# Two score products instead of three in the differential heads of a two-layer encoder, by rows copied between partitions

## The chip, the cores and the metric

The kernel runs on one core of a Trainium2 chip. The metric is the device time of one execution in microseconds (us). The kernel before took 2270.39 us (median of three executions, 2268.04 to 2270.62).

## The reference

Two layers (`L`) are applied with the same weights to two requests of 512 positions and width 1024. Per layer:

```
h = rms(x) * attn_norm;  z = h @ w_in                  # dq, dk, dv, c_q, c_kv, k_pe
dq, dk = rope(dq), rope(dk)                            # 4 heads, 2 components of 64 each
p = softmax(dq_c . dk_c / 8), c = 0, 1;  a = p_0 - lam * p_1
y_diff = rms(a @ dv) * subln                           # differential attention, 4 heads
y_mla = latent attention from c_q, c_kv, k_pe          # 4 heads, 128 + 64 wide
x = x + [y_diff, y_mla] @ w_o
x = x + (silu(h' @ w_gate) * (h' @ w_up)) @ w_down     # h' = rms(x) * ffn_norm
```

## The kernel before

All products are float32 in two parts: `x = hi + lo`, where `hi` is the rounded value and `lo` what is left. `product` (line 526) makes a product of three matmuls, hi·hi, hi·lo and lo·hi (lines 528, 529 and 530), added up in one PSUM bank. ScalarE makes the `hi`, VectorE the `lo`.

A layer does its attention for request 0, then for request 1 (a half each, called l and b in the code; there are four), and then the feed-forward part for both. Each engine does a half in an order written out by hand: `TENSOR_ORDER`, `SCALAR_ORDER` and `VECTOR_ORDER` (lines 71 to 108). An engine takes its steps strictly in that order and waits in each for semaphores. The steps that matter here:

- `P q1` is the projection of the queries of head 1, 8 products or 24 matmuls of 128x512. `Pa` and `Pb` are its two halves of 12 matmuls. `RP` (VectorE, line 1904) rotates its result into `r1` in four operations, `RH` (ScalarE, `rope_his`, line 1437) makes the `hi` part, `RL` (VectorE, `rope_los`, line 1920) the `lo` part.
- `S i` are the scores of a block of 128 queries (line 1140): for i below 16, differential head i // 4, its two components as two products of 128x512, so six matmuls. `MX i` (VectorE, line 2043) takes their row maxima, `EX i` (ScalarE, line 1476) their exponentials, `CB i` (VectorE, line 1994) puts the two components together, `T i` transposes on TensorE, `TH i` and `TL i` split that into hi and lo, `A a` applies it to the values. `S 16` to `S 31` are the latent heads. The score banks are three: a score waits for the exponential of the third one before it.
- `RQ`, `ST`, `RB` and `AP` belong to the norms of the heads' outputs.

A head's q and k projections come out with their 128 rows in four blocks of 32: component 0 first half, component 1 first half, component 0 second half, component 1 second half (`_pair`, line 2380). The queries of component c are kept in `qd[..][c]` as hi and lo with the rows of the other component at zero (a mask in `RH` and `RL`); the keys are kept once, in `kd` as hi and lo. So in each score matmul half of the 128 rows are zeros on the query side.

Weights come in DMAs of 1 MB (`w<-parked`, line 619) on SyncE's queue, each when a slot comes free. In the first half of layer 0 they come raw and are split by ScalarE and GpSimd while the half runs (`slot_hi` on line 1519, line 864). At the ninth chunk of a request 1 half, SyncE also stores request 0's `x` in one DMA of 2 MB (`keep_x`, line 636). ScalarE issues five DMAs, all in the first 16 us.

Of the kernel before, what the change touches and what calls it, by code (L numbers as in the profile page):

```python
# [66 lines left out]
def order(text):  # L67
# [4 lines left out]
    V | P q0 | P k0 | P q1 | S 0 | Pa k1 | S 1 | Pb k1 | T 0 | S 2 | Pa q2 | S 3 | T 1 | Pb q2 | Pa k2 | S 4 | T 2 | A  # L72
    0 | S 5 | Pb k2 | T 3 | Pa q3 | A 1 | S 6 | T 4 | Pb q3 | ST y0 | S 7 | T 5 | P k3 | S 8 | T 6 | Pa kpe | A 2 | S
    9 | Pb kpe | T 7 | RB y0 | Pa ckv | S 10 | A 3 | T 8 | S 11 | Pb ckv | T 9 | ST y1 | S 12 | T 10 | Pa cq0 | RB y1
    | S 13 | Pa cq1 | ST ckv | T 11 | Pb cq0 | S 14 | RB ckv | Pb cq1 | S 15 | ST cq | A 4 | T 12 | RB cq | T 13 | A 5
    | T 14 | P kn0 | P pe0 | P qn0 | T 15 | ST y2 | A 6 | A 7 | S 16 | P vm0 | S 17 | P vm1 | S 18 | P vm2 | RB y2 | P
    vm3 | T 16 | P kn1 | ST y3 | P qn1 | S 19 | P kn2 | RB y3 | S 20 | P pe1 | S 21 | T 17 | S 22 | P qn2 | T 18 | A 8
    | S 23 | P kn3 | P oa0 | T 19 | P qn3 | T 20 | A 9 | S 24 | S 25 | S 26 | S 27 | T 21 | P oa1 | S 28 | T 22 | P
    oa2 | T 23 | A 10 | S 29 | T 24 | S 30 | A 11 | T 25 | P oa3 | T 26 | P oa4 | T 27 | S 31 | A 12 | T 28 | A 13 |
    ST n | T 29 | P oa5 | T 30 | P oa6 | T 31 | A 14 | A 15 | P oa7 | P ob0 | P ob1 | P ob2 | RB n | P ob3 | P ob4 | P  # L80
    ob5 | P ob6 | P ob7
""")
SCALAR_ORDER = order("""
    V | RH q0 | RH k0 | EX 0 | EX 1 | RH q1 | TH 0 | EX 2 | TH 1 | RH k1 | EX 3 | TH 2 | EX 4 | RH q2 | EX 5 | TH 3 |
    YC 0 | TH 4 | RH k2 | EX 6 | RH q3 | TH 5 | EX 7 | TH 6 | EX 8 | RH k3 | TH 7 | EX 9 | EX 10 | SH y0 | TH 8 |
    YC 1 | TH 9 | EX 11 | LC ckv | TH 10 | EX 12 | RH kpe | SH y1 | TH 11 | EX 13 | EX 14 | SH ckv | LC cq0 | LC cq1 |
    TH 12 | EX 15 | TH 13 | SH cq | YC 2 | PH kn0 | TH 14 | PH qn0 | TH 15 | RH pe0 | EX 16 | PH vm0 | PH vm1 |
    PH vm2 | YC 3 | PH vm3 | PH kn1 | SH y2 | EX 17 | TH 16 | PH qn1 | EX 18 | EX 19 | SQ 0 | PH kn2 | SQ 1 | TH 17 |
    SH y3 | EX 20 | SQ 2 | TH 18 | PH qn2 | RH pe1 | PH kn3 | EX 21 | TH 19 | PH qn3 | EX 22 | EX 23 | EX 24 | TH 20 |
    YC 4 | EX 25 | EX 26 | TH 21 | TH 22 | EX 27 | TH 23 | TH 24 | SQ 3 | SQ 4 | YC 5 | TH 25 | EX 28 | TH 26 |  # L90
    EX 29 | EX 30 | SQ 5 | SQ 6 | TH 27 | SQ 7 | SN 0 | TH 28 | SN 1 | SN 2 | TH 29 | EX 31 | SN 3 | SN 4 | SN 5 |
    TH 30 | YC 6 | TH 31 | YC 7 | SN 6 | SN 7
# [40 lines left out]
def numbered(names):  # L133
    return {n: i for i, n in enumerate(names)}
# [4 lines left out]
ROPED = numbered([s[1] for s in VECTOR_ORDER if s[0] == "RP"])  # L139
ROPE_SPLITS = numbered([(n, c) for n in ROPED for c in range(2 if n[0] in "qp" else 1)])  # L140
# [130 lines left out]
def encoder_trunk(nc, xT, watt, wffn, tables, gains, lam, out):  # L271
    with ExitStack() as ctx:
        KB = 1024
# [67 lines left out]
        kd = [[at(f"kd{n}_{s}", [P, T], r_qk + (n * 12 + 8 + i * 2) * KB, F32R)  # L341
               for i, s in enumerate(("hi", "lo"))] for n in range(2)]
# [65 lines left out]
        def sem(name):  # L408
            return ctx.enter_context(nc.semaphore(name))
# [48 lines left out]
        s_rope_lo = Count(sem("rope_lo"), len(ROPE_SPLITS))  # L458
        s_latent = Count(sem("latent_copied"), len(LATENT))
# [544 lines left out]
        def _(pe):  # L1004
# [135 lines left out]
            def scores(l, b, i):  # L1140
                h, qt = i // NT, i % NT
                at_q = slice(qt * P, (qt + 1) * P)
                for c in range(2 if i < 16 else 1):
# [243 lines left out]
        def _(act):  # L1387
# [49 lines left out]
            def rope_his(l, b, name):  # L1437
# [365 lines left out]
        def _(dve):  # L1803
# [676 lines left out]
```

## Time and profile before

| | us |
|---|---|
| median of three executions | 2270.39 |
| the profiled execution | 2269.12 |
| its span, first to last instruction | 2267.3 |
| TensorE busy | 2232.9 (98%) |
| VectorE busy | 1803.7 (80%) |
| ScalarE busy | 984.7 (43%) |
| GpSimd busy | 990.3 (44%) |
| mean granted TensorE clock | 0.997 of full |

1.8 us of the profiled execution lie outside its span. The four attention halves begin near 0, 258, 1150 and 1374 us. Matmuls overlap in the pipeline: a duration of 0.39 us is not the time that one takes of TensorE; that is read from the distance of starts.

### The profile page before, as it was taken

To read this page: it belongs to the slowest core of one execution; us is meant where nothing else is said; L and a number is where in the kernel's file an instruction comes from. 1 tells how busy PE (TensorE), PEld (TensorE's weight loads), DVE (VectorE), ACT (ScalarE), POOL (GpSimd) and SP (SyncE) were. 2 spreads that over 40 slices of the span, in tenths; PEclk is the share of its full clock that TensorE was granted. 3 is DMA by queue.
4 is the path that set the end of the run, shared out by engine and by line. 5 is a ranking of instruction groups with operands and counts; after the bars stand their busy time and mean duration, and the time that the engine had idled before them with its cause. 6 is when DMAs were issued, how large, how long until landed. Compare 5 with 4: busy or idle time off the path is not lost.

```text
span 2267.3 us, 31231 instructions
## 1 busy us (share of the span) xinstructions
PE 2232.9 (98%) x10610; PEld 1858.7 (82%) x10610; DVE 1803.7 (80%) x2793; ACT 984.7 (43%) x1876; POOL 990.3 (44%) x686
## 2 busy tenths in 40 slices
PE   8999999999999999999999999999999999999998
PEld 6888888888888888888888888888888888888886
DVE  7998388888787878999958873988877676779988
ACT  4556144554444444443324541455444434444342
POOL 4314100124777777798700010001254455568893
PEclk9999999999999999999999999999999999999999
DMA  8633542233676766853243136312323232357522
GB/s 306 221 111 124 205 174 94 83 141 117 215 239 215 236 216 235 316 175 108 99 149 112 56 130 214 121 59 110 135 84 111 97 111 97 111 212 261 165 72 84
DMA packets 93463, 346.89 MB, mean 153 GB/s; under 512 B 9760, under 2 KB 9888, under 8 KB 74016
## 3 DMA queue, kind: packets, MB, share of 16 engines
q1 hardware_dynamic: 92624, 344.53, 43.7%
q8 instruction: 64, 1.05, 0.2%
q10 hardware_dynamic: 720, 0.86, 0.1%
q14 instruction: 55, 0.45, 0.1%
HBM read 237.35 MB, written 108.00 MB: 152 GB/s over the span
## 4 chain that ended last, share of the span: by engine, by line
PE 87%; DVE 6%; issue 1%; ACT 1%; POOL 0%; DVEq 0%; ACTq 0%; POOLq 0%
PE bank L528 28%; PE bank L530 27%; PE bank L529 27%; PE bank L1177 2%; PE bank L1015 1%; DVE x L2234 1%; DVE u L2200 1%; PE bank L1023 1%; PE bank L535 1%; PE bank L534 1%; DVE qpe L1928 1%; DVE aT_lo L2053 1%; DVE y_out L2341 0%; ACT aT_hi L1490 0%; DVE x L2242 0%
## 5 line engine op out<-in xcount | busy, mean ns | idle before, releaser
L905 POOL TENSOR_TENSOR slot<-raw,slot 128x512 fp32r<-128x512 f32 x160 | 223.4, 1400 | 234.4 <-ACT slot L1629 234.4
L528 PE MATMUL bank<-h_hi,slot 128*128 128x512 f32 x640 | 249.2, 389 | 0.0
L529 PE MATMUL bank<-h_lo,slot 128*128 128x512 f32 x640 | 249.1, 389 | 0.0
L530 PE MATMUL bank<-h_hi,slot 128*128 128x512 f32 x640 | 249.1, 389 | 0.0
L882 POOL TENSOR_TENSOR acc<-sq,zero 128x512 f32<-128x512 f32 x5 | 6.1, 1219 | 528.3 <-ACT sq L1418 528.3
L528 PE MATMUL bank<-u,slot 128*128 128x512 f32 x560 | 218.6, 390 | 1.1 <-DVE x L2234 1.1
L529 PE MATMUL bank<-u,slot 128*128 128x512 f32 x560 | 218.1, 389 | 0.0
L530 PE MATMUL bank<-u,slot 128*128 128x512 f32 x560 | 218.0, 389 | 0.0
L528 PE MATMUL bank<-h_hi,w 128*128 128x512 f32 x512 | 203.6, 398 | 0.0
L905 POOL TENSOR_TENSOR slot<-s_stage,slot 128x512 fp32r<-128x512 f32 x120 | 175.8, 1466 | 60.1 <-ACT slot L1629 58.6
L530 PE MATMUL bank<-h_hi,w 128*128 128x512 f32 x512 | 200.0, 391 | 0.0
L529 PE MATMUL bank<-h_lo,w 128*128 128x512 f32 x512 | 199.6, 390 | 0.0
L864 POOL TENSOR_TENSOR w<-raw,w 128x512 fp32r<-128x512 f32 x70 | 101.1, 1466 | 215.2 <-ACT w L1525 111.8
L529 PE MATMUL bank<-t_lo,slot 128*128 128x512 f32 x480 | 186.9, 389 | 0.0
L528 PE MATMUL bank<-t_hi,slot 128*128 128x512 f32 x480 | 186.9, 389 | 0.0
L530 PE MATMUL bank<-t_hi,slot 128*128 128x512 f32 x480 | 186.9, 389 | 0.0
L2234 DVE TENSOR_TENSOR x<-x,bank 128x512 f32<-128x512 f32 x280 | 175.3, 676 | 10.9 <-PE bank L530 10.6
L2200 DVE TENSOR_TENSOR u<-uf,u 128x512 fp32r<-128x512 f32 x140 | 170.5, 1257 | 13.8 <-ACT u L1659 13.8
L1482 ACT ACTIVATE e<-bank,mx 128x512 f32<-128x512 f32 x192 | 130.6, 686 | 99.1 <-DVE mx L2045 99.0
L2156 DVE TENSOR_TENSOR bank<-bank,snap 128x512 f32<-128x512 f32 x80 | 55.7, 696 | 143.7 <-PE bank L530 143.7
L1639 ACT ACTIVATE snap<-bank 128x512 f32<-128x512 f32 x160 | 95.5, 597 | 152.0 <-PE bank L530 151.9
L1629 ACT ACTIVATE slot<-raw 128x512 fp32r<-128x512 f32 x160 | 100.1, 627 | 97.1 <-DVE raw L2145 52.3
(261 smaller groups left out, 5931.6 us busy)
## 6 DMA issues: line engine op xcount, KB each, us to landing
w<-parked SPq DMA_DIRECT2D x81, 1024.0 KB, 4.9
raw<-in_wffn SPq DMA_DIRECT2D x112, 512.0 KB, 3.5
u_kept<-made SPq DMA_DIRECT2D x148, 256.0 KB, 2.8
uf<-u_kept SPq DMA_DIRECT2D x70, 512.0 KB, 5.7
parked<-w SPq DMA_DIRECT2D x27, 1024.0 KB, 6.3
parked<-p SPq DMA_DIRECT2D x27, 1024.0 KB, 4.9
raw<-in_watt SPq DMA_DIRECT2D x27, 512.0 KB, 4.3
praw<-in_watt SPq DMA_DIRECT2D x27, 512.0 KB, 5.8
```

Source lines behind the costliest of these rows:

```text
L528: nc.tensor.matmul(out_ap, lhs[0], rhs[0], start=first, stop=False, skip_group_check=joins)
L529: nc.tensor.matmul(out_ap, lhs[0], rhs[1], start=False, stop=False, skip_group_check=joins)
L530: return nc.tensor.matmul(out_ap, lhs[1], rhs[0], start=False, stop=last, skip_group_check=joins)
L864: last = nc.gpsimd.tensor_tensor(w[slot][1][:, cols], src[:, cols], w[slot][0][:, cols].bitcast(F32), ALU.subtract)
L905: nc.gpsimd.tensor_tensor(slot[i][:, 1, :], gate_source(i), slot[i][:, 0, :].bitcast(F32), ALU.subtract).then_inc(s_gate_lo.sem, 1)
L1177: last = nc.tensor.transpose(bank[5][:, k * P:(k + 1) * P], src[:, k * P:(k + 1) * P], ident[:])
L1482: nc.scalar.activation(e[e_buffer(ev)][:], bank[2 + ev % 3][:], ACT.Exp, bias=mx[:, ev:ev + 1], accum_out=ls[:, ev:ev + 1]).then_inc(s_exp ...
L1629: nc.scalar.activation(slot[i][:, 0, :], gate_source(i), ACT.Copy).then_inc(s_gate_hi.sem, 1)
L1639: nc.scalar.activation(snap[n][:], bank[4 * (1 - tt) + at][:], ACT.Copy).then_inc(s_snap.sem, 1)
L2156: nc.vector.tensor_tensor(z[:], z[:], snap[2 * b][:], ALU.add).then_inc(s_joined.sem, 1)
L2200: nc.vector.tensor_tensor(upair[d % 2][g][:, q, 1, :], upair_f[d % 2][g][:, q, 1, :], upair[d % 2][g][:, q, 0, :].bitcast(F32), ALU.subtra ...
L2234: nc.vector.tensor_tensor(xn, xn, at[m][:], ALU.subtract if g == N3 else ALU.add).then_inc(s_acc.sem, 1)
```

## The change

- The scores of a component become two matmuls (`doubled_product`). The `hi` queries of component c, own rows, are copied by DMA into the rows of the other component, which were zeros. The keys get a tile for each component, `kd[..][c]`: the `hi` keys in the component's own rows and, copied there by DMA, their `lo` part in the other rows. Then doubled hi queries times that tile is hi·hi + hi·lo, and the `lo` queries (own rows only) times it is lo·hi.
- `RH` of keys makes two tiles and not one. `RL` of keys writes one tile `k_low`, after both, and after the copies of the head before have landed.
- A new step `MV` on ScalarE waits for `RL` and issues four DMAs of 32 rows x 512 (64 KB) each: 8 tiles a half, 4 DMAs, 4 halves, 128 in all. `S 4h` waits for the copies of q and k of head h to land, instead of for `RL`.
- On TensorE `Pa k1` is moved ahead of `S 0`. On ScalarE `MV q0` and `MV k0` follow their `RH`; `MV q1` stands between `TH 1` and `RH k1`, `MV k1` after `EX 3`, `MV q2` between `TH 4` and `RH k2`. VectorE's order is unchanged.

```diff
 TENSOR_ORDER
-    V | P q0 | P k0 | P q1 | S 0 | Pa k1 | S 1 | Pb k1 | T 0 | S 2 | Pa q2 | S 3 | T 1 | ...
+    V | P q0 | P k0 | P q1 | Pa k1 | S 0 | Pb k1 | S 1 | T 0 | S 2 | Pa q2 | S 3 | T 1 | ...
 SCALAR_ORDER
-    V | RH q0 | RH k0 | EX 0 | EX 1 | RH q1 | TH 0 | EX 2 | TH 1 | RH k1 | EX 3 | TH 2 | EX 4 | RH q2 | EX 5 | TH 3 |
-    YC 0 | TH 4 | RH k2 | EX 6 | RH q3 | TH 5 | EX 7 | TH 6 | EX 8 | RH k3 | TH 7 | EX 9 | EX 10 | ...
+    V | RH q0 | MV q0 | RH k0 | MV k0 | EX 0 | EX 1 | RH q1 | TH 0 | EX 2 | TH 1 | MV q1 | RH k1 | EX 3 | MV k1 |
+    TH 2 | EX 4 | RH q2 | EX 5 | TH 3 | YC 0 | TH 4 | MV q2 | RH k2 | EX 6 | MV k2 | RH q3 | TH 5 | EX 7 | TH 6 |
+    MV q3 | EX 8 | RH k3 | TH 7 | EX 9 | MV k3 | EX 10 | ...
...
+        def doubled_product(pe, out_ap, lhs, rhs):
+            nc.tensor.matmul(out_ap, lhs[0], rhs, start=True, stop=False)
+            return nc.tensor.matmul(out_ap, lhs[1], rhs, start=False, stop=True)
...
+        def block_rows(c):
+            return [(own, 32 * (own // 32 ^ 1)) for own in (32 * c, 64 + 32 * c)]
...
-                            pe.wait_ge(s_rope_lo.sem, ...)
-                        last = product(pe, dst, [qd[h % 2][c][s][:, at_q] for s in range(2)],
-                                       [kd[h % 2][s][:] for s in range(2)], True, True)
+                            pe.wait_ge(s_q_moved[h % 2], moved_value(l, b, h))
+                            pe.wait_ge(s_k_moved[h % 2], moved_value(l, b, h))
+                        last = doubled_product(pe, dst, [qd[h % 2][c][s][:, at_q] for s in range(2)], kd[h % 2][c][:])
...
+            def move_rows(l, b, name):
+                n = int(name[1]) % 2
+                act.wait_ge(s_rope_lo.sem, s_rope_lo.half_at(l, b, ROPE_SPLITS[(name, 1)]))
+                for c in range(2):
+                    for own, other in block_rows(c):
+                        if name[0] == "q":
+                            tile_ = qd[n][c][0].bitcast(F32)
+                            act.dma_start(tile_[other:other + 32, :], tile_[own:own + 32, :]).then_inc(s_q_moved[n], 16)
+                        else:
+                            act.dma_start(kd[n][c].bitcast(F32)[other:other + 32, :], k_low.bitcast(F32)[own:own + 32, :]).then_inc(
+                                s_k_moved[n], 16)
...
+                if key_tile(name):
+                    h = int(name[1])
+                    dve.wait_ge(s_rope_hi.sem, s_rope_hi.half_at(l, b, q0 + 1))
+                    if h:
+                        dve.wait_ge(s_k_moved[(h - 1) % 2], moved_value(l, b, h - 1))
+                    nc.vector.tensor_tensor(k_low[:], r1[:], dst[0][:].bitcast(F32), ALU.subtract).then_inc(s_rope_lo.sem, 2)
+                    return
```

## Rows read from the trace of the kernel before

**Rows 1.** The page, busy time of each engine, its share of the span and its instructions.

```profile
PE 2232.9 (98%) x10610; PEld 1858.7 (82%) x10610; DVE 1803.7 (80%) x2793; ACT 984.7 (43%) x1876; POOL 990.3 (44%) x686
```

**Rows 2.** Busy time by stretch, 255 to 370 us, with granted clock, DMA share and GB/s.

```profile
255.00:370.00 115.00, 115.00 (x564) 96.52 (x563) 77.93 (x151) 39.40 (x88) 0.00 (x0) 1.00 0.47 163
```

**Rows 3.** Groups of instructions on TensorE, the first of the three score products.

```profile
L528 PE MATMUL bank<-kd_hi,qd_hi 128*128 128x512 f32 x128 | 52.4, 409 | 1.1 <-DVE kd_lo L1932 1.0
```

**Rows 4.** Busy time by stretch, products of line 528 alone, which stand every third.

```profile
258.16:270.40 12.24, 7.01 (x18) 3.38 (x18) 1.00 0.54 179
```

**Rows 5.** Timeline of TensorE, second request of layer 0: start, duration, idle before.

```profile
296.24 0.39 PE L528 MATMUL bank<-kd_hi,qd_hi 128*128 128x512 f32 x1
...
304.41 0.60 PE L1177 MATMUL bank<-ident,e 128*128 128x128 f32 x4
...
316.25 0.39 PE L528 MATMUL bank<-kd_hi,qd_hi 128*128 128x512 f32 x1
...
381.19 0.39 PE L528 MATMUL bank<-kd_hi,qd_hi 128*128 128x512 f32 x1
```

**Rows 6.** Timeline of ScalarE and VectorE, the same half.

```profile
293.86 0.63 ACT L1447 ACTIVATE kd_hi<-r 128x512 fp32r<-128x512 f32 x1 [4.10 <-DVE r L1918]
...
294.52 0.69 DVE L1932 TENSOR_TENSOR kd_lo<-r,kd_hi 128x512 fp32r<-128x512 f32 x1 [0.70 <-ACT kd_hi L1447]
301.20 1.37 DVE L2045 TENSOR_REDUCE mx<-bank 128x1 f32<-128x512 f32 x2 [0.74 <-PE bank L530]
302.93 0.75 DVE L2006 SCALAR_TENSOR_TENSOR e<-e,rc,e 128x512 f32<-128x512 f32 x1
312.73 1.28 DVE L2045 TENSOR_REDUCE mx<-bank 128x1 f32<-128x512 f32 x2
```

**Rows 7.** Issues of DMAs by ScalarE (timeline), then of all queues: KB, us to landing.

```profile
14.82 0.33 ACTq L1533 DMA_DIRECT2D e<-in_lam  x1
15.19 0.48 ACTq L1534 DMA_DIRECT2D cs<-in_tables  x1
...
g<-in_gains SPq DMA_DIRECT2D x1, 36.0 KB, 1.8
u_kept<-made SPq DMA_DIRECT2D x148, 256.0 KB, 2.8
ident<-in_tables ACTq DMA_DIRECT2D x1, 64.0 KB, 4.8
gsmall<-in_gains ACTq DMA_DIRECT2D x1, 4.0 KB, 7.2
```

**Rows 8.** Busy time by stretch, around the first scores and the second head.

```profile
295.00:297.00 2.00, 2.00 (x11) 1.65 (x10) 0.78 (x2) 0.00 (x0) 0.00 (x0) 1.00 1.00 340
317.00:319.00 2.00, 2.00 (x17) 1.83 (x16) 1.66 (x4) 0.75 (x2) 0.00 (x0) 1.00 0.37 156
```

**Rows 9.** Waits of VectorE, longest first, 317.2 to 384.5 us, then 74.5 to 141.5 us.

```profile
DVE aT_lo L2053 <- ACT aT_hi L1490: 3.6, 4, 1.4
DVE ms L1863 <- PE bank L1015: 1.2, 1, 1.2
...
DVE aT_lo L2053 <- ACT aT_hi L1490: 1.0, 2, 0.6
```

**Rows 10.** Timeline of TensorE, first request of layer 0, then of layer 1.

```profile
51.80 0.47 PE L528 MATMUL bank<-kd_hi,qd_hi 128*128 128x512 f32 x1 [0.96 <-DVE kd_lo L1932]
...
72.02 0.39 PE L528 MATMUL bank<-kd_hi,qd_hi 128*128 128x512 f32 x1
...
1174.41 0.47 PE L528 MATMUL bank<-kd_hi,qd_hi 128*128 128x512 f32 x1
```

**Rows 11.** Timeline of TensorE at 145 us, then busy time by stretch with granted clock.

```profile
145.58 0.65 PE L1023 MATMUL bank<-ident,yy 128*128 128x128 f32 x4 [2.19 <-DVE yy L1874]
...
147.00:150.00 3.00, 3.00 (x17) 3.00 (x16) 2.93 (x8) 2.45 (x5) 0.00 (x0) 0.54 0.98 401
150.00:152.00 2.00, 2.00 (x8) 1.57 (x8) 0.90 (x2) 1.24 (x3) 0.00 (x0) 0.83 0.81 340
```

More of the change, by code:

```diff
@@ L71 @@
 TENSOR_ORDER = order("""
[L72 to L80, printed above, removed]
@@ L81 @@
-    ob5 | P ob6 | P ob7
+    V | P q0 | P k0 | P q1 | Pa k1 | S 0 | Pb k1 | S 1 | T 0 | S 2 | Pa q2 | S 3 | T 1 | Pb q2 | Pa k2 | S 4 | T 2 |
+    A 0 | S 5 | Pb k2 | T 3 | Pa q3 | A 1 | S 6 | T 4 | Pb q3 | ST y0 | S 7 | T 5 | P k3 | S 8 | T 6 | Pa kpe | A 2 |
+    S 9 | Pb kpe | T 7 | RB y0 | Pa ckv | S 10 | A 3 | T 8 | S 11 | Pb ckv | T 9 | ST y1 | S 12 | T 10 | Pa cq0 |
+    RB y1 | S 13 | Pa cq1 | ST ckv | T 11 | Pb cq0 | S 14 | RB ckv | Pb cq1 | S 15 | ST cq | A 4 | T 12 | RB cq |
+    T 13 | A 5 | T 14 | P kn0 | P pe0 | P qn0 | T 15 | ST y2 | A 6 | A 7 | S 16 | P vm0 | S 17 | P vm1 | S 18 |
@@ new lines @@
+    P vm2 | RB y2 | P vm3 | T 16 | P kn1 | ST y3 | P qn1 | S 19 | P kn2 | RB y3 | S 20 | P pe1 | S 21 | T 17 | S 22 |
+    P qn2 | T 18 | A 8 | S 23 | P kn3 | P oa0 | T 19 | P qn3 | T 20 | A 9 | S 24 | S 25 | S 26 | S 27 | T 21 | P oa1 |
+    S 28 | T 22 | P oa2 | T 23 | A 10 | S 29 | T 24 | S 30 | A 11 | T 25 | P oa3 | T 26 | P oa4 | T 27 | S 31 | A 12 |
+    T 28 | A 13 | ST n | T 29 | P oa5 | T 30 | P oa6 | T 31 | A 14 | A 15 | P oa7 | P ob0 | P ob1 | P ob2 | RB n |
+    P ob3 | P ob4 | P ob5 | P ob6 | P ob7
@@ L89 @@
[L89 to L92, printed above, removed]
+    V | RH q0 | MV q0 | RH k0 | MV k0 | EX 0 | EX 1 | RH q1 | TH 0 | EX 2 | TH 1 | MV q1 | RH k1 | EX 3 | MV k1 |
@@ L93 @@
+    RH pe1 | PH kn3 | EX 21 | TH 19 | PH qn3 | EX 22 | EX 23 | EX 24 | TH 20 | YC 4 | EX 25 | EX 26 | TH 21 | TH 22 |
+    EX 27 | TH 23 | TH 24 | SQ 3 | SQ 4 | YC 5 | TH 25 | EX 28 | TH 26 | EX 29 | EX 30 | SQ 5 | SQ 6 | TH 27 | SQ 7 |
+    SN 0 | TH 28 | SN 1 | SN 2 | TH 29 | EX 31 | SN 3 | SN 4 | SN 5 | TH 30 | YC 6 | TH 31 | YC 7 | SN 6 | SN 7
 """)
@@ L139 @@
 ROPED = numbered([s[1] for s in VECTOR_ORDER if s[0] == "RP"])
-ROPE_SPLITS = numbered([(n, c) for n in ROPED for c in range(2 if n[0] in "qp" else 1)])
+ROPE_SPLITS = numbered([(n, c) for n in ROPED for c in range(1 if n == "kpe" else 2)])
 PLAIN = numbered(["dv0", "dv1", "dv2", "dv3"] + [s[1] for s in VECTOR_ORDER if s[0] == "PL"])
@@ L340, in encoder_trunk @@
                 for i, s in enumerate(("hi", "lo"))] for c in range(2)] for n in range(2)]
-        kd = [[at(f"kd{n}_{s}", [P, T], r_qk + (n * 12 + 8 + i * 2) * KB, F32R)
-               for i, s in enumerate(("hi", "lo"))] for n in range(2)]
+        kd = [[at(f"kd{n}{c}", [P, T], r_qk + (n * 12 + 8 + c * 2) * KB, F32R) for c in range(2)] for n in range(2)]
+        k_low = at("k_low", [P, T], r_s + 6 * KB, F32R)
         cq = [[at(f"cq{n}_{s}", [P, T], r_qk + (n * 4 + i * 2) * KB, F32R)
@@ L458, in encoder_trunk @@
         s_rope_lo = Count(sem("rope_lo"), len(ROPE_SPLITS))
+        s_q_moved = [sem(f"q_high_rows_doubled{n}") for n in range(2)]
+        s_k_moved = [sem(f"k_low_rows_placed{n}") for n in range(2)]
         s_latent = Count(sem("latent_copied"), len(LATENT))
@@ L543, in rope_target, with key_tile, moved_value @@
                 return [qpe[2 * n], qpe[2 * n + 1]], 2
-            return (qd[n % 2], 0) if name[0] == "q" else ([kd[n % 2]], None)
+            return (qd[n % 2], 0) if name[0] == "q" else (kd[n % 2], None)
+        def key_tile(name):
+            return name[0] == "k" and name != "kpe"
+        def moved_value(l, b, h):
+            return 4 * 16 * ((l * B + b) * (H // 2) + h // 2 + 1)
+        def block_rows(c):
+            return [(own, 32 * (own // 32 ^ 1)) for own in (32 * c, 64 + 32 * c)]
         def plain_target(name):
@@ L1446, in rope_his @@
                 for c, d in enumerate(dst):
-                    nc.scalar.activation((d if name[0] == "p" else d[0])[:], r1[:], ACT.Copy, scale=1.0 if scale is None else
+                    nc.scalar.activation((d if name[0] == "p" or key_tile(name) else d[0])[:], r1[:], ACT.Copy, scale=1.0 if scale is None else
                                          masks[:, scale + c:scale + c + 1]).then_inc(s_rope_hi.sem, 1)
+            def move_rows(l, b, name):
[9 more added lines that the diff above has]
+                                s_k_moved[n], 16)
             def latent_copy(l, b, name):
@@ L1560, in _ @@
                             rope_his(l, b, what)
+                        elif kind == "MV":
+                            move_rows(l, b, what)
                         elif kind == "LC":
```

9 lines of the change are left out of this document (4 added, 5 removed).

## The prediction, made before the changed kernel was run

> **What bounds the kernel now.** I read the page first, for who is busy. TensorE is busy for 98% of the span [rows 1], and in the stretch with request 1's first scores it never stops [rows 2]. So a matmul taken away is worth its full time as long as nothing else gets in front. The time of a 128x512 matmul comes from starts, not from durations: 18 products, three matmuls each, in 12.24 us [rows 4] is 0.227 us a matmul. Then I followed the timeline of one half, the second request of layer 0, because what the change moves is order and latency. There TensorE goes from `S 0` at 296.24 to `S 15` at 381.19 without a gap that matters [rows 5]. But VectorE runs beside it nearly as full: in the 67 us from 317.2 its two largest waits come to 3.6 + 1.2 = 4.8 us, and in the same part of the first half (74.5 to 141.5) the largest is 1.0 us [rows 9]. So there are two engines at their limit, each in a fixed order, and the change relieves only one.
>
> **What is removed.** The three score groups have 128 matmuls each [rows 3], and one of the three goes: 128 x 0.227 = 29.0 us, 7.2 us a half (32 matmuls), 0.45 us for each `S`. This is the whole prize, 1.3%. VectorE loses nothing: it still does two `RL` operations for q and one for k, and all maxima.
>
> **What is added: the first scores.** A time below is that of the half of rows 5 and 6, and "late" is against it. `RL k0` runs at 294.52 for 0.69 us, after one `hi` copy of 0.63 us [rows 6]. With two copies (the second some 0.5 us more) it ends at 295.75. Then `MV k0` issues four DMAs. Two ScalarE issues stand 0.37 us apart, lasting 0.33 and 0.48 us [rows 7]: I take 0.37 each, so the last starts 1.1 us after the first. How long a 64 KB copy within SBUF takes no row shows. From below it is bounded by 1.8 us (36 KB, a quiet time) and from above by 7.2 us (4 KB, issued by ScalarE behind others in the crowded first microseconds). A quiet time I price at 2.4 us, between the 1.8 and the 2.8 of 256 KB stores; a crowded one at 4.8 us from the first of the four issues, which is what 64 KB issued by ScalarE took in a crowd [rows 7]. At this place the DMA engines are full, share 1.00 [rows 8], with a 1 MB weight load and the 2 MB store in flight. So `S 0` comes at 295.8 + 4.8 = 300.6. `Pa k1`, moved ahead, is the cover: 12 matmuls, 2.7 us, to 298.96. The rest, 1.6 us, TensorE stands still, and `S 0` is 4.4 us late (2.7 of that for work moved, not lost).
>
> **The swap's own price: T 0.** Before, half a projection lay between `S 1` and `T 0`. Now `Pb k1` comes ahead of `S 1`, and nothing lies between. `T 0` needs `CB 0`, which VectorE does after `MX 1`, so after `S 1`. New: `S 0` 0.9 us, `Pb k1` 2.7 us, `S 1` from 304.2 to 305.1. `MX 1` ended at 301.20 + 1.37 = 302.57, 2.25 us after `S 1` began at 300.32; with shorter scores about 1.8 us, so 306.0, 3.4 us late. `CB 0` ended 1.1 us after it [rows 6]: `T 0` goes at 307.1 instead of 304.41 [rows 5]. TensorE waits 2.0 us.
>
> **Head 1.** VectorE's work from `MX 1` to `MX 3` (two `CB`, `RL q1`, `MX 2`, `TL 0`, `RP k1`, `CB 2`, `RL k1`) is serial and nearly gapless, so `MX 3`, which ended at 312.73 + 1.28 = 314.0 [rows 6], ends at 317.4. On ScalarE `MV q1` puts 1.5 us of issues ahead of `RH k1`, which then makes two copies; by my count of the order that fits just before `CB 2` ends, and costs nothing. `MV k1` stands behind `EX 3`, which waits for `MX 3`: first issue 317.45, last 318.55, landed at 320.95 at the quiet price (the share falls to 0.37 at 317 [rows 8]). `S 4` was at 316.25 [rows 5]; it is 4.7 us late. Queued behind it are `T 2`, `A 0` and all of TensorE's half, and on VectorE `MX 4`.
>
> **Winning it back.** From `S 4` to `S 15` are 12 score steps of 0.45 us: 5.4 us. Against that, `MV q2` puts 1.5 us ahead of `RH k2`, and this time VectorE stands waiting for it, in front of `TL 4`, `RP q3`, `MX 7` and `CB 6`; I make `T 6` 0.8 us late from it. The copies of heads 2 and 3 are issued two or more score steps with their projections ahead of `S 8` and `S 12`, and cost TensorE nothing; their second `hi` copies lie in idle time of ScalarE (43% busy [rows 1]), and would cost VectorE 0.5 us each without it. So the half ends at +4.7 + 0.8 - 5.4 = +0.1 us. That VectorE lets TensorE win this back is not sure: it can itself make up only about its waits, 4.8 us and some smaller ones.
>
> **The other halves.** The second request of layer 1 has the same traffic and the same distances: +0.1. In the first request of layer 1 no 2 MB store is in flight, so I take the quiet price; but there `S 0`, at 1174.41 [rows 10], follows `RL k0` at once, so all of the new chain is late: 0.4 us net for the second `hi` copy, 1.1 for the issues, 2.4 to land, 3.9 us in sum, against 4.4 above, and the half ends near -0.3. In the first half of all, TensorE already waits 0.96 us for `RL k0`, at 51.80, and `S 4` follows at 72.02 [rows 10]. With `RL k0` ending near 52.3 and 3.5 to 4.8 us for the four copies, `S 0` comes at 56 or later; the same chain gives `MX 1` 3.4 us and `MX 4` some 5 us late. VectorE has hardly a wait to make that up [rows 9], as its operations are stretched beside GpSimd's splits: I keep +4 (between +1.6, what the shorter scores alone would leave of a 7 us late `S 4`, and +5).
>
> **The sum** is +0.1 + 0.1 - 0.3 + 4 = +3.9 us on the profiled execution's 2269.12, so 2273.0. That execution lies 1.3 us under the median 2270.39, and on the median it is 2274. About 0.2% (4.5 us) is what a measurement of this kernel can tell from no change, so this is just within no change.
>
 The new waits of 2 to 4 us stand between full stretches of projections and not amid small transposes, so the sum has nothing for them; the other end is 1.7 us for each of up to 8. The Trainium skill, "TensorE: Matmul & The Clock Gate", section "Part 1: The HAM clock gate", says that the array's clock is halved after idling and given back by activity. By that rule the change would pay at each wait; its price is the rival below.
>
> **Rivals.**
> - **The copies land early and VectorE keeps up (faster).** At 1.8 us a copy, and less of a crowd, `S 0` waits nothing and `S 4` is about 2.5 us late; in the three later halves that is -2.3 us each, and without the wait at `T 6` -3. If VectorE's order had more slack than I see, the prize counts in full but for `T 0`: 29.0 - 4 x 2.0 = 21, so 2249. For it: TensorE's 98%. Against: rows 9. I give it 0.25, at about 2258.
> - **Copies land late in the queues' crowd (slower).** Its place is `S 0` and `S 4` of each half, its price up to 7.2 - 2.4 = 4.8 us at each. If both copies take 5 us and more, a half loses some 4 us beyond the forecast: 2274 + 16 = 2290. It decides from about 3.5 us a copy at `S 4`. For it: the 4.8 and 7.2 us rows. Against: at 317 the crowd is thinning. 0.17.
> - **The clock falls at the new waits (slower).** 1.7 us x 4 to 8 = 7 to 14 us: 2281 to 2288. 0.13.
> - That the change does not cut the matmuls is excluded by the code: the loop has two calls where it had three.
>
> **How the numbers follow.** The trade as I worked it out has 0.45, with a range of its own of 2263 to 2281 (0.05 faster, 0.25 same, 0.15 slower). The early case gives 0.21 faster and 0.04 same, the late one 0.14 slower and 0.03 same, the clock 0.09 slower and 0.04 same. Together faster 0.26, same 0.36, slower 0.38. The range 2255 to 2290 takes in the clock's 14 us, the late copies, and the early case short of its full 2249.
>
> **What would show it.** Right: 256 matmuls in score groups instead of 384; TensorE waits on a DMA once before `S 0` and once before `S 4` in each half, 1 to 4 us each; some 2 us in front of `T 0` on VectorE's `CB`; VectorE waiting for `kd` before `RL k2`; the distance `S 4` to `S 15` shorter than the 64.94 us of before by 4 to 5 us; the first half worse than the others. Wrong: no wait at `S 4`, then the early case; copies of 4 us and more there, the late one; a granted clock near 0.5 in the stretches behind the waits, the clock; `S 4` to `S 15` no shorter than before, then VectorE bounds it and the loss is larger than I say.

## The result and the profile after

| | before | after |
|---|---|---|
| median, us | 2269.22 (4 runs, 2267.76 to 2270.62) | 2333.22 (4 runs, 2332.74 to 2334.05) |
| span of the profiled execution, us | 2267.3 | 2331.7 |
| mean granted TensorE clock | 0.997 | 0.982 |
| TensorE busy | 98% | 96% |

The ratio is 1.028 with a 95% interval of 1.0265 to 1.030: slower by 64 us. The forecast was 2274 with a range of 2255 to 2290: a change of +4 us and no visible change, where +64 came. The 64 us are more than twice the whole prize of 29.0, and with the prize itself some 93 us of new cost have to be found.

The page of the changed kernel, part 1, answers to [rows 1]:

```profile
PE 2231.4 (96%) x10482; PEld 1848.6 (79%) x10482; DVE 1803.4 (77%) x2793; ACT 993.6 (43%) x1892; POOL 989.5 (42%) x686
```

128 matmuls are gone (10610 to 10482), yet TensorE is busy for almost as long: 2231.4 against 2232.9 us, where 29.0 us less were due. So two things happened, and the page shows both: the remaining work became slower by some 27 us, and on top TensorE stands still for a further 66 us (span less busy time is 100.3 us, before 34.4). The two together are the 93.

The waits of TensorE in the changed kernel (what it waited for, then total us, times, longest) name the second part:

```profile
PE bank L541 <- DMA kd<-k_low: 51.0, 8, 9.6
PE bank L1195 <- DVE e L2046: 10.1, 8, 2.0
...
PE bank L541 <- ACT e L1513: 3.9, 6, 1.3
...
PE bank L530 <- POOL w L882: 2.2, 1, 2.2
```

Before, the same view has 0.4 us for the second line, nothing for the third, 0.2 for the fourth and 1.0 in front of the first score product (the 0.96 of [rows 10]). The copies of the keys hold TensorE exactly eight times, twice a half, for 6.4 us on average: 51.0 us. The forecast had 1.6 us at `S 0` and some 2 more at `S 4`.

The timeline of TensorE in the second request of layer 0, changed kernel (start, duration, then in brackets the idle time before and its releaser). It answers to [rows 5]:

```profile
333.29 0.77 PE L541 MATMUL bank<-kd,qd_hi 128*128 128x512 f32 x1 [7.92 <-DMA kd<-k_low]
...
341.47 0.66 PE L1195 MATMUL bank<-ident,e 128*128 128x128 f32 x4 [2.04 <-DVE e L2046]
...
357.32 0.76 PE L541 MATMUL bank<-kd,qd_hi 128*128 128x512 f32 x1 [4.69 <-DMA kd<-k_low]
```

The three lines are `S 0`, `T 0` and `S 4`. `T 0` waits 2.04 us where 2.0 was forecast. `S 0` waits 7.92 where 1.6 was. To compare timelines I take the start of the same step in both traces; the difference is its lateness. In the kernel before, `V` starts at 7.8, 258.2, 1134.7 and 1372.9 us (so the third half begins near 1135 and not near 1150). In us:

| step | L0, req. 0 | L0, req. 1 | L1, req. 0 | L1, req. 1 |
|---|---|---|---|---|
| `V` (the half begins) | 0.7 | 26.3 | 40.3 | 50.3 |
| `S 0` | 13.4 | 37.1 | 46.9 | 60.8 |
| `S 3` | 13.8 | 36.7 | 47.7 | 61.2 |
| `S 4` | 24.5 | 41.1 | 51.7 | 65.1 |
| `S 5` | 26.0 | 43.1 | 53.5 | 66.3 |
| `S 15` | 26.0 | 40.7 | 50.8 | 63.4 |
| end of the half | 26.3 | 40.2 | 50.3 | 63.0 |

The halves add 25.6, 14.0, 10.1 and 12.7 us. The loss arises at `S 0` and at `S 4`, a little more at `S 5`, and after that at most 3.3 us come back. In the first half 2.9 us more are lost at `S 8`, of which 1.3 us are a wait for an exponential.

**Why the copies were late.** First the ScalarE timeline of that half, then what the view of line 1478 (the copies of the keys) says for `MV k0`, in 320 to 336 us: min/median/max of the issues' durations in ns, and from issue to landing in us.

```profile
316.88 2.45 ACTq L1476 DMA_DIRECT2D qd_hi<-qd_hi  x4
320.11 1.15 ACT L1465 ACTIVATE kd<-r 128x512 fp32r<-128x512 f32 x2 [4.10 <-DVE r L1951]
322.09 4.29 ACTq L1478 DMA_DIRECT2D kd<-k_low  x4
335.25 0.69 ACT L1513 ACTIVATE e<-bank,mx 128x512 f32<-128x512 f32 x1 [13.98 <-DVE mx L2085]
```

```profile
L1478 ACTq DMA_DIRECT2D kd<-k_low x4: 514/1124/1436, 322.1 to 324.9; - x4
...
  PE bank L541: 7.9, 1
...
DMA to landing us min/median/max: 7.4/8.2/8.2
```

Two terms were mis-sized at once. Four issues take ScalarE 2.45 us in a quieter time and 4.29 in a crowd, where the forecast had 4 x 0.37 = 1.5. And each copy lands 7.4 to 8.2 us after its own issue; the forecast had 4.8 us from the first issue to the last landing, and that came to 324.9 + 8.2 - 322.1 = 11.0. The same view of `MV k1`, 350 to 360 us, when the large transfers are through:

```profile
L1478 ACTq DMA_DIRECT2D kd<-k_low x4: 513/610/613, 353.3 to 355.2; - x4
...
  PE bank L541: 4.7, 1
...
DMA to landing us min/median/max: 1.9/2.0/2.1
```

Such a copy lands in 2.0 us, less than the 2.4 that were assumed. Yet `S 4` still waits 4.7 us, since the chain of `MX 3`, four issues behind `EX 3` and the landing stands alone on the path. The crowd is seen on SyncE's queue of the changed kernel, at 317.62 (the store of `x`, 2 MB) and at 322.69 (a weight load, 1 MB), the second in the midst of the copies:

```profile
317.62 0.52 SPq L656 DMA_DIRECT2D x_kept<-x  x1
322.69 0.32 SPq L637 DMA_DIRECT2D w<-parked  x1
```

**Why the remaining work became slower.** Busy time by stretch in the changed kernel: the stretch; its length; busy time of PE, PEld, DVE, ACT and POOL; then granted clock, DMA share and GB/s.

```profile
326.00:328.00 2.00, 0.00 (x0) 0.00 (x0) 0.00 (x0) 0.00 (x0) 0.00 (x0) 1.00 0.99 409
328.00:330.00 2.00, 0.00 (x0) 0.00 (x0) 0.00 (x0) 0.00 (x0) 0.00 (x0) 0.83 0.98 382
330.00:332.00 2.00, 0.00 (x0) 0.00 (x0) 0.00 (x0) 0.00 (x0) 0.00 (x0) 0.50 0.78 257
...
334.00:336.00 2.00, 2.00 (x7) 1.52 (x6) 1.31 (x2) 0.75 (x2) 0.00 (x0) 0.50 0.00 0
336.00:338.00 2.00, 2.00 (x10) 1.67 (x9) 0.07 (x1) 0.81 (x3) 0.00 (x0) 0.96 0.00 0
```

TensorE stops at 325.4, the clock falls to 0.50, its 1.2 GHz level, while it stands, and `S 0` and what follows run at that level until about 336. Nine such stretches lie in the differential parts of the four halves, 61.2 us long together; in each of them the granted clock is 0.50, and TensorE is busy in them for 39.3 us. The two of this half:

```profile
329.30:336.10 6.80, 2.81 (x7) 2.26 (x8) 1.38 (x2) 0.78 (x2) 0.00 (x0) 0.50 0.34 115
356.60:363.40 6.80, 6.08 (x22) 5.46 (x23) 3.14 (x7) 3.15 (x7) 0.00 (x0) 0.50 0.02 6
```

39.3 us of products at half pace have cost 19.7 us more than at full. Two more stretches lie elsewhere: 6.8 us at 168.9 (5.3 busy), for which the kernel before has 3.4 us at 147.2 [rows 11], and 3.4 us at 2309.0, for which it has none. They add 2.7 us by the same reckoning. Together that is most of the 27 us by which the busy time is too long; the rest is not broken down.

### The profile page after: what moved, and what is told of

The parts are those of the page before. It is cut to its first block and busy times, and to the rows that moved or that the text cites. A ratio compares the mean times of both kernels' runs of the same rounds, so it can differ in the third digit from the quotient of the medians.

```text
span 2331.7 us, 31143 instructions
## 1 busy us (share of the span) xinstructions
PE 2231.4 (96%) x10482; PEld 1848.6 (79%) x10482; DVE 1803.4 (77%) x2793; ACT 993.6 (43%) x1892; POOL 989.5 (42%) x686
## 5 line engine op out<-in xcount | busy, mean ns | idle before, releaser
L530 PE MATMUL bank<-h_hi,w 128*128 128x512 f32 x512 | 206.5, 403 | 2.2 <-POOL w L882 2.2
L532 PE MATMUL bank<-h_hi,w 128*128 128x512 f32 x512 | 202.1, 395 | 0.0
L2085 DVE TENSOR_REDUCE mx<-bank 128x1 f32<-128x512 f32 x192 | 125.8, 682 | 67.1 <-PE bank L542 61.5
```

The source lines that it names most:

```text
L530: nc.tensor.matmul(out_ap, lhs[0], rhs[0], start=first, stop=False, skip_group_check=joins)
L532: return nc.tensor.matmul(out_ap, lhs[1], rhs[0], start=False, stop=last, skip_group_check=joins)
L2085: nc.vector.tensor_reduce(mx[:, ev:ev + 1], bank[2 + ev % 3][:], AX_X, ALU.max, negate=True).then_inc(s_max.sem, 1)
```

## The experiments

Ten kernels, each run beside the kernel before, which took 2269.3 to 2270.5 us. All but one were executed once, with a profile. Nine executions of the kernel before lay between 2267.6 and 2270.7 us, so a difference of 3 us between two single times says little; the lateness of the halves and the waits say more. Unless stated, each edit is against the changed kernel.

**1. The swap alone**, in the kernel before. TensorE's order only:

```diff
-    V | P q0 | P k0 | P q1 | S 0 | Pa k1 | S 1 | Pb k1 | T 0 | ...
+    V | P q0 | P k0 | P q1 | Pa k1 | S 0 | Pb k1 | S 1 | T 0 | ...
```

> The kernel before with nothing changed but TensorE's order: Pa k1 ahead of S 0, Pb k1 ahead of S 1. Three products a component and no copies. Theory Q (the copies' delivery is what costs: issues of 0.6 us, landings of 2 to 9 us, with the clock that falls while TensorE waits): the swap alone costs only the 2.0 us wait before T 0 in each half, 4 x 2.0 = +8 us, so 2277 us. Theory V (VectorE's fixed order is the bound, and whatever makes it late early in a half stays): each half loses 3 us or more, 2281 us and up. If the swap costs nothing, 2269.

Measured 2279.71 us, 9.4 above the kernel before beside it. Its waits of TensorE have one new line:

```profile
PE bank L1177 <- DVE e L2006: 8.0, 5, 1.9
```

8.0 us, as forecast for `T 0` (4 x 2.0), and the time is longer by all of it. The halves end 3.2, 5.4, 7.0 and 10.7 us late, and from `S 4` on the lateness within a half stays as it is to 0.4 us: what is lost at `T 0` is never won back. TensorE is busy 98% of the time here and has no slack in which to make up. The time lies between the two theories (2277, and 2281 up). What is above 8.0 is clock: there are three stretches of 3.4 us at 0.50, all full of products, where the kernel before has one. The first stands in front of every step that was moved:

```profile
29.20:32.60 3.40, 3.40 (x10) 2.62 (x10) 3.04 (x9) 1.57 (x3) 2.19 (x2) 0.50 0.87 328
```

The traces of experiments 6 and 10 have such a stretch at 28.8 us too, of 3.4 and 6.8 us, and the others have none there. So a single time can carry 1.7 to 3.4 us that its edit has not caused.

**2. The changed kernel with the swap undone.** The old order of TensorE, all else as changed.

> The changed kernel with TensorE's old order (S 0 ahead of Pa k1, S 1 ahead of Pb k1). The time at which the first copies have landed does not depend on the order. Theory Q: S 0 starts at the same time after RL k0, now with no projection half done before it, so TensorE waits 2.7 us longer at S 0 (about 10.6 us in request 1 of layer 0) and does not wait 2.0 us at T 0: +0.7 us a half, plus up to 1 us of low clock, 2333 + 3 to 7 = 2336 to 2340. Theory V: VectorE sees MX 0 at the same time and MX 1 at 2.7 us earlier, so the half gains 2 us or more: 2325 or less.

Measured 2328.43, 4.8 us less than the changed kernel. The waits for the copies rise from 51.0 to 64.0 us and those at `T 0` fall from 10.1 to 2.0:

```profile
PE bank L541 <- DMA kd<-k_low: 64.0, 8, 13.0
...
PE bank L1195 <- DVE e L2046: 2.0, 4, 0.8
```

This lies between the two theories (2336 to 2340, and 2325 or less). In waits the half key projection covers more (13.0 us) than it costs at `T 0` (8.1), as meant. The time is shorter all the same, because the products themselves became faster. The page has

```profile
PE 2225.4 (96%) x10482; PEld 1843.9 (79%) x10482; DVE 1802.2 (77%) x2793; ACT 994.1 (43%) x1892; POOL 990.2 (43%) x686
```

6.0 us less busy time than the changed kernel with the same 10482 matmuls, at an idle time that is 0.9 us longer. Of its busy time 37.4 us lie in stretches at 0.50, against 49.9 in the changed kernel, and half of that difference is 6.3 us. So with the swap more of the work falls into the stretches at 0.50; why it does was not tested.

**3. The crowd taken away.** The store of `x` and the load of the next request's `x` go to a later chunk.

```diff
-X1_AFTER = 12
+X1_AFTER = 20
...
-                        if b == 1 and j == 9:
+                        if b == 1 and j == 20:
```

> The changed kernel with two large transfers moved away from the copies: the 2 MB store of x from chunk 9 to chunk 20 (both request 1 halves, it was in flight at k0's copies), and the 2 x 1 MB load of request 1's x from chunk 12 to chunk 20 (first half, in flight at k1's copies). Theory Q: the copies of k0 in the request 1 halves, that landed 8.2 us after their issue, land some 4 us sooner (4.3 us is what they took in layer 1's first half with a 1 MB load beside them), and those of k1 in the first half land in 2 to 3 us instead of 7: 4 + 4 + 4.5 us, with some clock 2333 - 13 to -16 = 2317 to 2320. Theory V: VectorE-bound, most of it is not returned: 2328 or more.

Measured 2317.62, 15.6 us less. The same `MV k0` as above, without the 2 MB store in front of it:

```profile
L1478 ACTq DMA_DIRECT2D kd<-k_low x4: 514/610/613, 318.3 to 320.2; - x4
...
  PE bank L541: 3.4, 1
...
DMA to landing us min/median/max: 1.9/4.9/5.5
```

Issues are down to 0.61 us, landings from 8.2 to 4.9, the wait from 7.9 to 3.4. Layer 1, request 1 does the same (7.9 to 5.0, wait 7.6 to 3.7), and in the first half the landing at `S 4` falls from 7.0 to 2.1 (wait 9.6 to 7.2). All waits for the copies fall from 51.0 to 39.6 us. What stays in each half are the weight loads of 1 MB, beside which a copy takes 4 to 5 us. So the big transfers account for 15.6 of the 64 us, and the copies by DMA are too dear without them too.

**4. The same copies made by ScalarE.** Each DMA is replaced by an activation that writes 32 rows into another block of 32 partitions:

```diff
-                            act.dma_start(tile_[other:other + 32, :], tile_[own:own + 32, :]).then_inc(s_q_moved[n], 16)
+                            nc.scalar.activation(qd[n][c][0][other:other + 32, :], qd[n][c][0].bitcast(F32)[own:own + 32, :],
+                                                 ACT.Copy).then_inc(s_q_moved[n], 1)
```

and the like for the keys; all orders as changed.

> The changed kernel with each of the 128 copies made as one ScalarE operation on 32 partitions (a Copy that writes 32 rows further up or down) in place of a DMA, in the same places of ScalarE's order; no DMA queue and no landing. ScalarE's time for four is about 2.4 us, what the four issues take now. Theory Q: S 0 waits nothing, S 4 1 to 2 us, T 0 2.0 us; of 7.2 us a half 3 to 4 are kept: 2269 - 12 to -16 = 2253 to 2257. Theory V: VectorE's lateness after MX 1 and before RL k2 remains and eats the rest: 2265 to 2275. Were the loss none of the copies' delivery, it would stay near 2333.

Measured 2291.90: 41.3 us less than with DMAs, 21.6 more than before. Both theories missed it. The waits and the ScalarE timeline around `MV k0`:

```profile
PE bank L541 <- ACT kd L1478: 19.1, 6, 4.6
PE bank L1195 <- DVE e L2046: 9.3, 6, 2.0
```

```profile
303.73 2.59 ACT L1478 ACTIVATE kd<-k_low 32x512 fp32r<-32x512 f32 x4 [0.83 <-DVE k_low L1961]
```

Four copies take 2.59 us of ScalarE, about what the four issues alone took (2.45), and the data is there at the end of it. But between `S 3` and `S 4` each half still loses 5.6, 4.3, 4.3 and 4.3 us: `MV k1` stands behind `EX 3`, which waits for `MX 3`. Here there is no DMA left to blame: with copies by ScalarE this is the fault of the order, and I had counted all of it to the DMA.

**5. The same, with the orders mended.** TensorE's old order, and on ScalarE:

```diff
-    ... EX 1 | RH q1 | TH 0 | EX 2 | TH 1 | MV q1 | RH k1 | EX 3 | MV k1 | TH 2 | EX 4 | RH q2 | EX 5 | TH 3 | YC 0 | TH 4 | MV q2 | RH k2 | ...
+    ... EX 1 | RH q1 | TH 0 | EX 2 | MV q1 | TH 1 | RH k1 | MV k1 | EX 3 | TH 2 | EX 4 | RH q2 | EX 5 | TH 3 | MV q2 | YC 0 | TH 4 | RH k2 | ...
```

with `EX 8` ahead of `MV q3`.

> The copies as ScalarE operations (as in the run before, 2291.9 us), with TensorE's old order (no swap) and the copy steps moved to idle places of ScalarE's order: those of q1 ahead of TH 1, those of k1 right after RH k1 and ahead of EX 3, those of q2 ahead of YC 0, those of q3 after EX 8. In the run before, a half lost 4.3 to 5.6 us between S 3 and S 4, where S 4 waited for k1's copies behind EX 3, and 2.0 us at T 0. Theory P (what the halves lose is the place of the copies in ScalarE's order, in front of TensorE): S 4 waits under 1 us, T 0 not at all, 4 x (4 + 1.2) us back: 2268 to 2273. Theory V (VectorE's order is full and bounds the rest): 2280 or more.

Measured 2273.37, 18.5 us less than experiment 4 and at the upper end of what theory P gave. The three later halves each gain now (the halves end 8.5, 5.7, 5.1 and 3.7 us late), the first loses 8.5. At `T 0` 0.8 us of waiting are left of 9.3, and for the copies TensorE waits:

```profile
PE bank L541 <- ACT kd L1478: 17.4, 8, 5.4
```

**6. Keys sooner.** On top of 5, `RL` of a key waits for the first of the two `hi` tiles alone, and `S` of component 0 waits for its own copies only:

```diff
-                            pe.wait_ge(s_k_moved[h % 2], moved_value(l, b, h))
+                            pe.wait_ge(s_k_moved[h % 2], moved_value(l, b, h) - 2 * (1 - c))
...
-                    dve.wait_ge(s_rope_hi.sem, s_rope_hi.half_at(l, b, q0 + 1))
+                    dve.wait_ge(s_rope_hi.sem, s_rope_hi.half_at(l, b, q0))
```

(the waits for the second tile move to `rope` and `move_rows`).

> The same, and k's low part is made after the first high copy and not after both (the second runs beside it), and the scores of component 0 wait for that component's copies alone. S 0 is the place: it comes 0.5 us sooner by the first, and its first product another 1.2 us by the second. Theory P: 4 x 0.5 to 4 x 1.7 us below the kernel without this, 2262 to 2270. Theory V: no change from it.

Measured 2266.48, 6.9 us less than 5. Waits for copies are at 8.1 us (17.4 in 5), those of score products for exponentials at 6.0 (3.5 in 5). The halves end 9.1, 4.5, 2.2 and -2.5 us late: three halves gain 4.6, 2.3 and 4.7 us, and the first gives back 9.1. Of the half that gained least the ScalarE timeline shows why:

```profile
1178.84 2.58 ACT L1479 ACTIVATE kd<-k_low 32x512 fp32r<-32x512 f32 x4 [0.30 <-DVE k_low L1963]
1181.44 1.28 ACT L1514 ACT_TABLE_LOAD   x1
1182.74 0.69 ACT L1514 ACTIVATE e<-bank,mx 128x512 f32<-128x512 f32 x1
```

A load of the exponential's table (1.28 us) stands before `EX 0`. In the kernel before it lay in idle time, at 1173.56, and now the copies have pushed it into the chain. Experiment 9, which loads the table early, bears this out: this half gains 4.1 us there.

**7. TensorE kept busy.** The DMA kernel with useless products into a bank that is free then, ahead of the waits of `S 0` and `S 4`, which compute nothing that is used. Their number (15 to 40) fills each wait as measured.

```diff
+                            if c == 0 and h < 2:
+                                ...
+                                for n in range(WARM[(l, b, h)]):
+                                    nc.tensor.matmul(bank[tail][:], h0[0][:, 0, 0:P], h0[0][:, 0, :], start=True, stop=True)
```

> The changed kernel with products of no use (128x512, one weight, into a free bank) put in front of the waits of S 0 and S 4, 15 to 40 of them, as many as fill most of the wait that stands there (3.9 to 9.6 us). What it leaves the same are the waits; what it changes is what TensorE does in them. Theory C (each wait also costs the clock: in the changed kernel the granted clock is 0.50 for 3 to 7 us behind 8 waits): S 1 and S 5 come 1.5 to 2.5 us sooner behind each, 8 x 1.5 to 2 = 12 to 16 us: 2317 to 2321. If the low clock is hidden by VectorE anyway: 2333.

Measured 2322.04, 11.2 us less (a little under the 12 to 16 expected), with a mean granted clock of 0.994 for 0.982. The copies land as before (8.0 us at `MV k0` of the second half), and the idle 51.0 us have become 6.6 of idling plus the useless products. In the stretch where the clock was 0.50:

```profile
320.00:340.00 20.00, 17.46 (x74) 13.94 (x73) 8.66 (x16) 4.71 (x11) 0.00 (x0) 0.95 0.62 235
```

So the clock is a cost of its own, 11 us of the 64 at least. The page shows that it is somewhat more:

```profile
PE 2263.3 (98%) x10687; PEld 1875.5 (81%) x10687; DVE 1798.9 (78%) x2793; ACT 993.4 (43%) x1892; POOL 990.7 (43%) x686
```

The 205 useless matmuls are 205 x 0.227 = 46.5 us, so the useful ones take 2216.8 us, 14.6 less than in the changed kernel. The idle time is 43.4 us shorter (56.9 for 100.3); the useless products outlast it by 3.1 us, and 14.6 - 3.1 = 11.5 is the difference of the two spans.

**8. The issues alone**, in the kernel before: the `MV` steps stand in their new places and issue 128 DMAs of the same size into a scratch tensor in DRAM, for which TensorE never waits.

```diff
+                        act.dma_start(scratch[copies[0]], src[own:own + 32, :]).then_inc(..., 16)
```

> The kernel before (three products, its order on TensorE), with the 128 DMAs of the change issued at the same places of ScalarE's order, from the same rows into unused memory, and nobody waiting for them to land but what would overwrite their source. So it has the price of the issues, 4 x 0.61 us in ScalarE's order for each of 8 tiles a half, without that of landing. Theory Q (delivery to S 0 and S 4 is the loss): the issues cost little, 1 to 2 us a half in front of RH k1 and RH k2: 2274 to 2280. Were the issues themselves, by making ScalarE late, the main loss: 2300 or more.

Measured 2275.37, 4.9 us over the 2270.45 beside it. The halves end 5.7, 5.9, 5.9 and 6.1 us late, so all of it arises in the first half. ScalarE's issuing as such costs the later halves nothing. These DMAs end in DRAM and not in SBUF, so the run tells of the issues and not of how the real copies land.

**9. Only where it pays.** Experiment 6, but the first half of layer 0 stays as it was (three products, one `hi` tile, no copies), and a one-element exponential at `V` of layer 1 loads the table early:

```diff
+                        if l == 0 and b == 0:
+                            last = product(pe, dst, [qd[h % 2][c][s][:, at_q] for s in range(2)],
+                                           [kd[h % 2][s][:] for s in range(2)], True, True)
+                        else:
+                            last = doubled_product(pe, dst, [qd[h % 2][c][s][:, at_q] for s in range(2)], kd[h % 2][c][:])
...
+                            if l and b == 0:
+                                nc.scalar.activation(loaded[:], ones[:, 0:1], ACT.Exp)
```

> The kernel with ScalarE's copies and the keys sooner (2266.5 us), with the first of the four halves as in the kernel before (three products, no copies), and a one-element Exp at the start of layer 1's first half, so that the table that ScalarE needs for its exponentials is loaded there and not between the copies of k0 and EX 0. In the run before, the first half lost 9.1 us and the three later ones gained 4.6, 2.3 and 4.7 us. Theory P (each half stands for itself): +0 - 4.6 - 2.3 - 4.7 = -11.6 us, and 1 to 2 us more in layer 1's first half from the table: 2257 to 2259. If the first half's loss is only moved to later halves: 2264 or more.

Measured 2258.29 us, median of 5 (2256.84 to 2259.59), against 2269.32, median of 9: ratio 0.9953, 95% interval 0.994 to 0.9967. This is faster than both kernels, by 0.5% against the one before. The group of its first score products:

```profile
L541 PE MATMUL bank<-kd,qd_hi 128*128 128x512 f32 x96 | 40.0, 417 | 5.7 <-ACT kd L1490 4.0 <-ACT e L1525 1.7
```

96 matmuls fewer are worth 96 x 0.227 = 21.8 us, and 11.0 us are left (11.8 between the spans of the profiled executions). 4.4 us go in idle time of TensorE (38.8 for 34.4), in which the new waits of 4.0 us for copies and 1.7 for exponentials are contained. The other 5.6 us are busy time, which fell by 16.2 and not by 21.8; of these, 1.7 us are a stretch near the end, at which the kernel before had its full clock:

```profile
2232.90:2236.30 3.40, 3.40 (x12) 2.64 (x11) 2.28 (x7) 1.23 (x2) 1.27 (x1) 0.50 0.00 0
```

Where the remaining 3.9 us went, the runs do not show. The first half ends 0.1 us late, as it should, and the next two gain 4.6 and 4.1 us.

**10. DMAs in the best order.** Orders as in 5, transfers moved as in 3, but copies by DMA.

> The change with its DMAs, with all that helped elsewhere: TensorE's old order, ScalarE's copy steps in the idle places, the 2 MB store and the load of request 1's x moved away (2317.6 us with the last alone). Theory Q: what is left is the delivery, four issues of 0.61 us in a row and 2.0 us or more to land, 4.5 us in all where the operations on ScalarE need 2.4: S 0 waits some 5 us and S 4 1 to 2 us a half. From 2317.6: S 4's wait of some 4 us to 1.5, the swap's 1.2, some clock, 4 x 4 = -16: 2299 to 2305, still slower than before. If the order was the fault, and not the DMAs, it comes near the 2273.4 us of the operations.

Measured 2317.56, no better than experiment 3 alone, and 13 to 19 us above what I expected. The waits:

```profile
PE bank L541 <- DMA kd<-k_low: 44.8, 8, 13.8
```

In the second request of layer 0 the copies of `k1`, now issued earlier, fall among the weight loads and land in 4.9 us in place of 2.0: part of what the order gained the crowd took. The halves add 26.5, 7.3, 7.9 and 6.8 us, against 22.3, 8.6, 8.3 and 9.1 in experiment 3: the three later ones are a little better, the first is worse, and 3.4 us of that are a stretch of 6.8 us at 0.50 from 28.8 us on, before the first copy. Against experiment 5, which has the same orders with copies by ScalarE, the DMAs cost 2317.6 - 2273.4 = 44.2 us (3.4 of them that stretch), even with the large transfers out of the way. Merging the four copies of a tile into fewer DMAs was not tried, nor issuing them from another engine.

## Why the prediction was wrong

**The delivery of the copies was mis-sized; this was the main error.** The step "a crowded one at 4.8 us from the first of the four issues" took the landing of a single transfer for that of four in a row, and the issue price from two issues at the start of the program (0.33 and 0.48 us [rows 7]). Measured: 0.61 us an issue, 1.1 in the crowd, and up to 8.2 us from each copy's own issue. By this `S 0` of the second half came 10.8 us late within the half and not 4.4. The upper bound, 7.2 us, was among my rows, from a transfer issued by ScalarE behind others in a crowd [rows 7], the very situation of `S 0`; I chose the middle one. And the bound was itself too low, since issues and landing add: 11.0 us from the first issue to the last landing. All in all TensorE waited 51.0 us for the copies, 12.6 of them in the second half, where the forecast had 1.6 and some 2. The Trainium skill ("DMA: Bandwidth & Descriptors", section "Issuing engines are not separate DMA queues") says that DMAs started by different engines run on the same 16 DMA engines and interleave. The traces agree: 8.2 us beside a 2 MB store, 4.9 without it (experiment 3), 2.0 when the large transfers are through. The same section of the Trainium skill calls the time to initiate a DMA usually small relative to the DMA itself. Here it was not: 4 x 0.61 = 2.4 us against 2.0 to land.

**The clock was left out of the sum.** That "the sum has nothing for them" was a choice against my own row: [rows 11] showed a fall to 0.54 after a wait of 2.19 us. The reason given, that the new waits stand between full stretches of projections, was no reason. TensorE had been fully busy up to 325.4 and the clock fell all the same. The windows above show a clock of 0.50 from 330 to 336 us, within and behind the wait, and one of 0.96 in 336 to 338, behind products. The rule that the prediction cited from the Trainium skill ("TensorE: Matmul & The Clock Gate", section "Part 1: The HAM clock gate"), halved after idling and given back by activity, agrees with that. The rival's price was near: 1.7 us x 8 = 14, and in experiment 7 the useful products take 14.6 us less and the time is 11.2 less. That it fits so well is in part luck, for the stretches last from 3.4 to 10.2 us and are filled differently.

**The winning back did not come.** From `S 4` to `S 15` 4 to 5 us were to be gained. Measured in the second half: 421.84 - 357.32 = 64.52 us against 64.94. The shorter scores are real, but the way from `S 4` to `S 5` grew by 2.0 us, with the clock at 0.50 behind the wait, and the 2.4 us that came back from `S 5` to `S 15` just pay for it. The prediction had named this sign, "`S 4` to `S 15` no shorter than before, then VectorE bounds it". The sign came, but the cause that it named is not the one. In experiment 7, with the clock kept up and the same work on VectorE, the same stretch takes 416.69 - 354.95 = 61.74 us, 3.2 less than before. In experiment 5, which has neither the DMAs nor this fall of the clock, it takes 60.88, 4.1 less, as forecast (4 to 5).

**The second half, summed:** 6.4 us at `S 0` (10.8 for 4.4), 1.3 at `S 3` (the lateness fell by 0.4 and not by the 1.7 forecast up to `T 0`), 2.4 at `S 4` (a rise of 4.4 for 2.0), 2.0 to `S 5`, and 1.7 from there to the end (-2.9 for -4.6, the 0.8 at `T 6` included). That is 13.8, and the half went from the forecast +0.1 to +14.0.

**The first half was the worst, as forecast, but at +25.6 and not +4.** Its two waits are the longest (8.8 and 9.6 us), copies landing in 6.5 and 7.0 us among the raw weights, parking stores and the loads of the next `x`. The forecast had landings of 3.5 to 4.8 us for all four. No experiment splits this half into its causes; in experiment 8, with the issues and their traffic alone, it ends 5.7 us late.

**Two rivals together.** The late copies and the slow clock were rivals with 0.17 and 0.13, each priced as if alone, and both came; the first feeds the second: with the long waits the trace has 49.9 us of products at 0.50, and in experiment 7, where the waits are filled, 16.7. Together they gave 16 + 14 us on 2274, so 2304: still 29 us short, because the late rival was priced at 4.8 us a place, without the longer issues and with no surcharge for the first half. The range ended at 2290, the price of the late copies alone.

**What was right.** 256 matmuls in score groups for 384; a wait on a DMA before each `S 0` and each `S 4`, and nowhere else; 2.0 us at `T 0`, and 8.0 us of waits for the swap in a kernel with nothing else changed; the worth of a matmul, since in the second half of experiment 9 the lateness falls by 4.4 us in the ten steps from `S 5` to `S 15`, 0.44 for each `S` where 0.45 was forecast; the copies of heads 2 and 3, for which TensorE never waits.

**The 64 us by cause, as far as runs show:** the copies' way by DMA in place of ScalarE is 41.3 us (experiment 4), in which the large transfers (15.6) and a part of the clock's 11.2 are contained (the mean granted clock is 0.991 there, for 0.982); the orders, swap included, 18.5 (5 against 4); the late keys 6.9 (6 against 5). These sum to 66.7, and experiment 6 is in fact 4.0 us below the kernel before. The sum holds for this order of steps only: with copies by DMA, experiment 10 against 3, the same orders gave nothing, or 3 us if its early stretch at 0.50 is taken off.

## What to carry to other kernels

- A small DMA on the critical path costs its issue on the engine that issues it, times their number, plus a landing that is set by whoever else is in the queues: 2.0 us with the large transfers through, 8.2 beside a 2 MB store. Price it at the worst landing in the trace from the last issue on, or move the rows with a compute engine that stands idle (43% busy here).
- A prize spread over a hundred matmuls must be set against each serial point it adds, together with the clock lost behind the wait. A TensorE that is busy 98% of the time does not win back what it lost in a wait.
- Leave a change out where it doesn't pay: three of the four halves gained and the first lost, and leaving the first alone made the difference between 2266.5 and 2258.3 us, with an early table load.

## What the hardware did that was not expected

- A DMA issue on ScalarE's queue took 0.61 us for 32 partitions x 512 in SBUF, and up to 1.77 us in a crowd. SyncE's issue of a 1 MB load took 0.32 us (at 322.69, above).
- An activation that writes 32 partitions into another block of 32 took 0.65 us (2.59 for four), and the four together are about as long as issuing four DMAs that do the same (2.45).
- The clock fell to 0.50 while TensorE stood still for 7.9 us in the midst of full work, and stayed there for the products behind it until about 336. In three of the twelve traces (experiments 1, 6 and 10) it also fell to 0.50 at 28.8 to 29.2 us, amid products, where the other nine ran at full clock.
